# Two weight pieces in another order on GpSimd, and a sum read from PSUM, in a hybrid attention and MoE block

## What is computed

```python
xn = rmsnorm(h, g_mix)
proj = xn @ w_in                     # q, k, v of two attentions, and the gates g_a, g_b
y_a = dilated_attention(...)         # 8 heads
y_b = nsa_attention(...)             # 8 heads, three branches
merged = (sigmoid(g_a) * (y_a @ w_branch_a)
          + sigmoid(g_b) * (y_b @ w_branch_b))
h = h + merged @ w_out
h = h + moe_ffn(rmsnorm(h, g_ffn), ...)      # 64 experts, 8 of them per token, one shared expert
h = h + (p @ w_ple) * sigmoid(rmsnorm(h, g_ple) @ w_ple_gate)
return rmsnorm(h, g_final)
```

## Time and profile before

| | us |
|---|---|
| median of 3 executions | 1152.1 (1151.97 to 1152.79) |
| profiled execution | 1154.9 |
| its span in the trace | 1153.1 |
| TensorE busy | 1087.6 (94%) |
| VectorE busy | 459.4 (40%) |
| GpSimd busy | 280.9 (24%) |
| mean granted clock of the core | 0.983 |

### The profile page before, as it was taken

The page is one execution under the profiler, slowest core; times in us unless marked ns, Lnnn a source line. Parts: engine busy times, 40 slices in busy tenths (PEclk is TensorE's granted clock), DMA queues, the critical chain, the costliest instruction groups (busy, mean ns, idle before and its releaser), DMA issues.

```text
span 1153.1 us, 19687 instructions
## 1 busy us (share of the span) xinstructions
PE 1087.6 (94%) x7927; PEld 630.1 (55%) x7928; DVE 459.4 (40%) x1032; ACT 283.1 (25%) x653; POOL 280.9 (24%) x210
## 2 busy tenths in 40 slices
PE   6999999999998989999999999999999989999796
PEld 4888787777676879753333333333333333333375
DVE  5444655545446663553222341221211111111787
ACT  5023333333334611121111111111111111111523
POOL 3622534333323422111111111111111111110043
PEclk9999999999998999999999999998999999999999
DMA  9611222111110533599999999999999999988771
GB/s 368 255 54 38 67 62 69 60 55 56 56 28 29 200 129 138 222 373 336 413 427 429 424 421 423 422 422 408 421 415 422 420 396 424 413 365 318 314 312 74
DMA packets 50379, 307.84 MB, mean 267 GB/s; under 512 B 10352, under 2 KB 11248, under 8 KB 31088
## 3 DMA queue, kind: packets, MB, share of 16 engines
q1 hardware_dynamic: 38480, 273.00, 59.0%
q0 software_dynamic: 11808, 33.57, 7.3%
HBM read 290.28 MB, written 25.69 MB: 274 GB/s over the span
## 4 chain that ended last, share of the span: by engine, by line
PE 70%; DMA 19%; issue 5%; DVE 2%; POOLq 1%; POOL 1%; DVEq 0%; SPq 0%; ACT 0%
PE bank L1546 17%; PE bank L462 16%; DMA sb_gate_up<-in_w_gate_up 16%; PE bank L1572 7%; PE bank L1123 4%; PE bank L1113 4%; DMA sb_down<-in_w_down 3%; PE bank L471 3%; PE bank L495 3%; PE bank L526 3%; PE bank L1150 2%; PE bank L508 2%; PE bank L1536 2%; PE bank L1090 1%; PE bank L548 1%
## 5 line engine op out<-in xcount | busy, mean ns | idle before, releaser
L1546 PE MATMUL bank<-sb_gate_up,sb_xgT 128*32 128x512 f32 (+1 forms) x2384 | 296.1, 603 | 21.2 <-DMA sb_gate_up<-in_w_gate_up 20.8
L462 PE MATMUL bank<-sb_x_hl,sb_w_hl 128*128 128x512 f32 x768 | 192.6, 403 | 10.5 <-DVE sb_x_hl L588 10.5
L1546 PEld LDWEIGHTS bank<-sb_gate_up,sb_xgT 128*32 128x32 f32 (+1 forms) x2384 | 88.9, 114 | 197.2 <-issue 193.7
L462 PEld LDWEIGHTS bank<-sb_x_hl,sb_w_hl 128*128 128x128 f32 x768 | 142.5, 191 | 57.9 <-issue 24.2
L1572 PE MATMUL bank<-sb_down,sb_work 128*32 128x512 f32 (+1 forms) x1192 | 149.3, 595 | 4.1 <-DMA sb_down<-in_w_down 2.5
L1650 POOL DMA_INDIRECT expert_rows<-sb_rows_out,sb_work x41 | 42.6, 1039 | 452.9 <-DVE sb_rows_out L1724 452.9
L263 POOL TENSOR_TENSOR sb_w_hl<-sb_r,sb_w_hl 128x1024 fp32r<-128x1024 f32 x52 | 126.1, 2429 | 69.1 <-ACT sb_w_hl L1252 46.2
L1734 DVE TENSOR_TENSOR sb_work<-sb_work,bank 128x256 f32<-128x256 f32 x41 | 17.3, 422 | 268.2 <-ACT sb_work L1772 268.2
L1572 PEld LDWEIGHTS bank<-sb_down,sb_work 128*32 128x32 f32 (+1 forms) x1192 | 44.0, 112 | 81.2 <-issue 77.8
L672 DVE CUSTOM_DVE_ANT_0 sb_h<-bank,sb_bias 128x128 f32<-128x128 f32 (+3 forms) x96 | 43.4, 489 | 112.2 <-PE bank L495 111.7
L1772 ACT ACTIVATE sb_work<-bank 128x256 f32<-128x256 f32 x41 | 15.8, 385 | 293.9 <-PE bank L1546 293.9
(11 more groups left out here) (255 smaller groups left out, 1294.4 us busy)
## 6 DMA issues: line engine op xcount, KB each, us to landing
sb_gate_up<-in_w_gate_up SPq DMA_DIRECT2D x55, 2048.0 KB
sb_down<-in_w_down SPq DMA_DIRECT2D x64, 1024.0 KB
sb_r<-in_w_front SPq DMA_DIRECT2D x54, 512.0 KB, 3.6
sb_gate_up<-in_w_gate_up SPq DMA_DIRECT2D x18, 1024.0 KB
sb_rows<-expert_rows SPq DMA_DIRECT2D x6, 2048.0 KB, 16.7
sb_gateT<-in_cmp_w SPq DMA_DIRECT2D x2, 2048.0 KB, 13.6
sb_rows<-expert_rows SPq DMA_DIRECT2D x3, 1024.0 KB, 8.2
sb_y<-in_x_T SPq DMA_DIRECT2D x4, 512.0 KB, 7.1
```

The lines of the kernel that those rows point to most:

```text
L462: last = nc.tensor.matmul(out[:, :], w6_hl[:, slot_at[n], zw, k, :], x_hl[:, zx, k, :], start=k + i == 0, stop=k == KD - 1 and i == 2)
L1546: last = nc.tensor.matmul(bank[BH][rows, :], xgT[:, k, rows], gate_up[slot_of[r]][:, k, :, :], start=k == 0, stop=k == KD - 1)
```

## The change

In `front_gpsimd` the last two of the first five branch pieces change places: piece 42 (m = 4) is split before piece 41 (m = 3), and piece 41 waits for the last scaling (`F["scaled"]`) and no more for the last biasing. The counts of `s_split` that the products and loads wait for are adapted: TensorE waits for count 43 for m = 3 (42 before), and the load of piece 46 (which follows piece 41 in its raw buffer) for 43 (42 before). In `middle_vector` the first product of each m is written back to its PSUM bank in place of `sb_gateT`, the sum reads it from there, and the rest of block m stands directly behind the sum of block m, not behind the sum of block m+1.

```diff
@@ load_piece
             if n >= 5:
-                sp.wait_ge(s_split, n - 4)
+                sp.wait_ge(s_split, n - 4 if n != WM_PIECE + 8 else n - 3)
@@ front_gpsimd
-            for m in range(5):
+            for m in (0, 1, 2, 4, 3):
                 n = WM_PIECE + m
                 pool.wait_ge(s_rawp[buf_of[n]], landed[n])
                 if SLOT_WM[m] < 5:
                     pool.wait_ge(F["done"], read_by[last_in[SLOT_WM[m]]])
                 else:
-                    pool.wait_ge(F["biased"], 2 * NU)
+                    pool.wait_ge(F["scaled"], 2 * NU)
                 split_piece(pool, buf_of[n], SLOT_WM[m])
@@ middle_tensor
             for m in range(KD):
-                pe.wait_ge(s_split, WM_PIECE + m + 1)
+                pe.wait_ge(s_split, WM_PIECE + (m + 1 if m != 3 else 5))
@@ middle_vector
                 dve.wait_ge(M["sig"], m + 1)
                 dve.wait_ge(M["merged_pe"], m + 1)
-                nc.vector.tensor_tensor(gateT[:, m, :], gateT[:, m, :], bank[2 * (m % 4)][:, :], ALU.mult)
+                nc.vector.tensor_tensor(bank[2 * (m % 4)][:, :], gateT[:, m, :], bank[2 * (m % 4)][:, :], ALU.mult)
                 nc.vector.tensor_tensor(gateT[:, KD + m, :], gateT[:, KD + m, :], bank[2 * (m % 4) + 1][:, :], ALU.mult)
                 dve.drain()
-                nc.vector.tensor_tensor(mT[:, m, :], gateT[:, m, :], gateT[:, KD + m, :], ALU.add).then_inc(M["merged"], 1)
-                if m:
-                    rest_of_m(m - 1)
-            rest_of_m(KD - 1)
+                nc.vector.tensor_tensor(mT[:, m, :], bank[2 * (m % 4)][:, :], gateT[:, KD + m, :], ALU.add).then_inc(M["merged"], 1)
+                rest_of_m(m)
```

## The result

| | before | after |
|---|---|---|
| median, us | 1152.0 | 1140.9 (1139.3 to 1141.3) |
| ratio to before | | 0.9901, interval 0.9882 to 0.9921 |
| profiled execution, and its span | 1154.9, 1153.1 | 1140.4, 1138.6 |

The changed kernel is faster by 11.4 us (9.1 to 13.6). The forecast was 1139.5, with a range of 1137.5 to 1146.5, and the measured time lies inside it. One of the four executions after took 1556.9 at a mean granted clock of 0.747 (0.990 to 0.991 in the other three); the range, the ratio and its interval leave it out, the median of four has it, and no run shows what slowed it.

What follows compares the result with a forecast made beforehand. TensorE was taken as the path, stalled at the attention's and merge's ends by VectorE instructions held by GpSimd. 5.9 + 0.6 + 4.8 + 1.3 = 12.6 us takes the median from 1152.1 to 1139.5, range 1137.5 to 1146.5.

Steps and rivals of the forecast that it cites:

- branch products start earlier: Attention's end: with the pieces moved, L1113 starts at 367.4 in place of 373.28, 5.9 us gained.
- they run at full clock: Branch products: 192 matmuls take 43.4 us in place of 44.05, 0.6 gained.
- the gap: Merge's end: TensorE's wait between branch products and output projection goes, 4.8 us gained.
- slow start of the output projection: Output projection: its first 12 matmuls take 1.38 us in place of 2.70 at clock 0.50, 1.3 gained.
- Part 1: Attention's end: moving pieces 41 and 42 frees VectorE's L698 and L701; gains 5.9 and 0.6 us.
- after three idles in 4 us: Attention's end: the clock dropped after three TensorE idles, of which one is left; argued against the clock falling again.
- Part 2: Merge: sum from PSUM and each rest behind its own sum; gains 4.8 and 1.3 us.
- Even with a blocked sum the rest would end at 5.4, just in time: Merge: with the sum still held by GpSimd, the rest ends 5.4 us after L1315's start; a block takes 5.4.
- The clock did not fall: Rival, attention's end: TensorE falls to 1.2 GHz near 363.5 all the same; gain 9.6, time 1142.5; chance 0.12.
- Neither half failed: Rival: piece 42 starts late, or the output projection still waits; gain 6.1 to 6.5, time 1146; chance 0.11.
- All arrived: Opposed rival: the expert weights' streaming start does not move, so nothing arrives at the end; time 1152; chance 0.04.
- slower: Rival, expert weights: their stream's rate falls 2.2%, gain gone; at 2.6% time is 1154; chance 0.04.

Runs made afterwards that it cites:

- order, late start: The changed kernel with piece 42 held until the last biasing; median 1145.0, ratio to before 0.9927.
- PSUM-sum run: The kernel before with only the merge's sum read from PSUM, the rest still behind the next block's sum; ratio 0.9993 (0.9981 to 1.0006).
- wait-only run: The kernel before with one edit: piece 41 waits for the last scaling, still ahead of piece 42; ratio 1.0012, 1.4 us slower.

## Why the prediction was right

By its own terms, from the profiles counted from T:

| step | predicted | measured |
|---|---|---|
| branch products start earlier | 5.9 | 5.64 |
| they run at full clock | 0.6 | 0.24 |
| the gap | 4.8 | 4.79 |
| slow start of the output projection | 1.3 | 1.35 |
| sum, at the experts' start | 12.6 | 12.2 |
| at the end of the span | 12.6 | 12.7 |

The four steps add up to 12.0; the other 0.2 is an overlap in the trace, whose matmul ends are modelled (after, the branch products' row ends 0.16 behind the start of the output projection). The profiled execution was forecast at 1142.3 and took 1140.4: the 1.8 by which T is earlier is no part of the change. The timed gain, 11.4, is 1.2 under the forecast, whose 12.6 lies inside the interval.

*Part 1.* L698 and L701 came free of GpSimd, and at the lengths forecast (0.16, 0.88). What frees them is that piece 42 runs early, not the order: held back, the same order gives 1.8 of the 5.6 ("order, late start": 14.8 in place of 16.5, where the untouched attention lies between 15.4 and 16.5). The 5.9 came out 0.26 too large, and the steps up to the handover show where. The last scaling ended 6.5 after T and not 6.3, since VectorE idles 0.43 before the last small multiplication, as it did before. Piece 41 and the first rest followed from there, and the rest ended 10.8 after T and not 10.7. From its end to the first branch product pass 0.13, which the forecast put at nothing. TensorE's own value products were finished 9.9 after T and not 10.2, but they were not what the start waited for.

The prediction's reading that the clock fell "after three idles in 4 us" is wrong. The view of windows of the profile before (columns as in the earlier trace rows):

```profile
362.00:364.00 2.00, 0.66 (x4) 0.42 (x4) 2.00 (x2) 0.63 (x2) 2.00 (x1) 0.89 0.00 0
364.00:366.00 2.00, 1.35 (x8) 1.02 (x10) 1.50 (x5) 0.20 (x1) 1.86 (x3) 0.50 0.02 4
```

The mean of 0.89 over 362 to 364 puts the fall at about 363.5, inside the second idle time (362.83 to 364.65), with only the 1.55 ahead of it. So the forecast that one idle time would not bring the clock down stood on less than it claimed, though it came true.

*The 0.6* was mis-sized. I took a rate from a count of matmuls in a stretch of the earlier trace rows whose ends cut matmuls, and such a count is too coarse for a term this small. The changed kernel runs the same 192 matmuls at full clock in 43.81, so the kernel before lost 0.24 of its 44.05.

*Part 2.* The gap went as forecast and by the edit that was priced as enough ("Even with a blocked sum the rest would end at 5.4, just in time"): the place of the rest alone leaves 0.20. The PSUM sum, whose 1.9 per block looked like the gain, shows no effect alone and adds slack to the other.

*Luck.* Both prices of the lower clock were read from one profile, which had the high one at the attention (16.5 to the branch products, where the same code needed 15.4 in the PSUM-sum run) and the low one at the output projection (1.35, where the other runs with a gap show 1.6 to 2.6). The two deviations have opposite signs. That the sum came out within 0.4 is in part luck.

*The rivals.* The clock did not fall, with idle times of 1.20 and 1.04 left. Neither half failed. All arrived: the way from the experts' start to the end is 637.3 before and 636.7 after. The stream of expert weights was not slower. The case of "slower" was not where I had put it: the wait-only run shows a nearer one, both pieces behind the scaling in the old order, 1.4 slower than before.

## What to carry to other kernels

When an instruction is many times its usual length, look for GpSimd at the same time, and move GpSimd's work to a stretch where VectorE reads PSUM or rests, not only past the place that suffers: work moved a little too late stalls the next two-input instruction, and a row of them one by one. Shortening a blocked instruction is worth nothing while the next one in the queue is blocked by the same neighbour; moving the one that is waited for ahead of it is. And a stall of TensorE of 4.2 to 4.8 us had a second price here, at the lower clock behind it, that differed from 1.3 to 2.6 between profiles.

## What the runs showed that was not expected

- How long the lower clock lasts after the same stall differs between executions: the 32 value products behind the untouched stall took 3.68 in the profile before, 3.58 with the rest's place alone and 2.54 in the PSUM-sum run; the output projection behind the untouched gap of 4.79 needed 93.7 to the experts in one profile and 94.9 in another. A single profile therefore shares a gain of 12 out between two places with an error of 1.2.
- T itself has two values, 354.8 to 355.3 and 356.3 to 356.7, in these profiles, whatever the kernel: some 1.6 that belong to the kernel's first 30 us, where the mean granted clock was 1.00 in the profiles with the early T and 0.94 in those with the late one. Two spans are not to be compared without it.
- VectorE and GpSimd take turns when both have a queue of instructions that hold each other: in the wait-only run each of the first four rests of y ends some 0.5 behind a GpSimd instruction. There VectorE did the eight rests of y in 10.92 (5.72 and 4.91 in others), with GpSimd's cast at 1.51 and its two subtractions at 5.41 (1.04 and 4.79 alone).
